# Moving six waits and taking the second block's norm squares to ScalarE in a two-block float32 kernel

## The reference

```
h = rms_norm(first_block(x));  h = layer_norm(h, ln_in)
for l in 0, 1:
    h = layer_norm(ALPHA * h + mixer(h), ln1[l])
    h = layer_norm(ALPHA * h + peer(h),  ln2[l])
layer_norm(x): mu = mean(x); var = mean((x - mu)^2); (x - mu) * rsqrt(var + 1e-5) * g + b
```

## Time and profile before

| | |
|---|---|
| median of 3 runs | 3114.88 us (3111.44 to 3116.8) |
| profiled execution | 3113.87 us |
| its span, first to last instruction | 3111.7 us |
| TensorE matmul busy | 3059.2 us, 98% |
| VectorE busy | 2120.8 us, 68% |
| ScalarE busy | 1488.1 us, 48% |
| GpSimd busy | 419.5 us, 13% |
| mean granted TensorE clock | 0.996 |
| DMA | 579.6 MB, mean 186 GB/s |

### The profile page before, as it was taken

The page is one execution under the profiler, slowest core; times in us unless marked ns, Lnnn a source line. Parts: engine busy times, 40 slices in busy tenths (PEclk is TensorE's granted clock), DMA queues, the critical chain, the costliest instruction groups (busy, mean ns, idle before and its releaser), DMA issues.

```text
span 3111.7 us, 59223 instructions
## 1 busy us (share of the span) xinstructions
PE 3059.2 (98%) x21073; PEld 2793.1 (90%) x21073; DVE 2120.8 (68%) x3732; ACT 1488.1 (48%) x2326; POOL 419.5 (13%) x246
## 2 busy tenths in 40 slices
PE   8999999999999999999999999999999999999998
PEld 8998899999888997899999978887899999988886
DVE  5567555555756557669788767776759977867776
ACT  4455444444644444444454445454434454545543
POOL 0001000000011002038700000001108810000000
PEclk9999999999999999999999999999999999999999
DMA  6543255455333553457765677774447765577775
GB/s 226 184 154 116 95 171 188 163 186 186 121 102 133 186 188 113 159 177 227 219 189 185 199 240 240 243 240 162 156 149 219 229 199 182 184 240 241 240 243 178
DMA packets 213024, 579.60 MB, mean 186 GB/s; under 512 B 23744, under 2 KB 88544, under 8 KB 212368
## 3 DMA queue, kind: packets, MB, share of 16 engines
q1 hardware_dynamic: 209504, 563.67, 54.8%
q0 software_dynamic: 3376, 13.94, 1.4%
HBM read 541.34 MB, written 36.18 MB: 186 GB/s over the span
## 4 chain that ended last, share of the span: by engine, by line
PE 87%; POOL 4%; DVE 4%; issue 3%; DMA 1%; ACT 1%; SPq 0%; POOLq 0%; ACTq 0%; DVEq 0%
PE work L667 40%; PE acc L690 33%; POOL wsp L640 3%; PE acc L752 3%; PE acc L1222 3%; PE acc L1089 2%; DVE wsp L417 1%; PE work L1123 1%; PE work L890 1%; PE work L904 1%; PE work L680 1%; DMA back<-acts_dram 0%; PE work L1010 0%; DVE st L2043 0%; PE work L816 0%
## 5 line engine op out<-in xcount | busy, mean ns | idle before, releaser
L667 PE MATMUL work<-xsp,wsp 128*128 128x256 f32 x12096 | 1502.5, 284 | 0.7 <-DVE wsp L417 0.7
L667 PEld LDWEIGHTS work<-xsp,wsp 128*128 128x128 f32 x12096 | 1472.2, 192 | 10.7 <-issue 3.0
L417 DVE TENSOR_TENSOR wsp<-ring,wsp 128x1024 fp32r<-128x1024 f32 x824 | 1011.8, 1229 | 569.1 <-ACT wsp L414 568.3
L414 ACT ACTIVATE wsp<-ring 128x1024 fp32r<-128x1024 f32 x944 | 994.3, 1054 | 648.1 <-PE work L667 352.3
L690 PE MATMUL acc<-wsp,hsp 128*128 128x512 f32 x4128 | 954.3, 390 | 4.6 <-DVE hsp L2312 4.4
L690 PEld LDWEIGHTS acc<-wsp,hsp 128*128 128x128 f32 x4128 | 770.3, 188 | 162.8 <-issue 6.2
L640 POOL TENSOR_TENSOR wsp<-ring,wsp 128x1024 fp32r<-128x1024 f32 x120 | 306.1, 2562 | 159.7 <-ACT wsp L414 159.5
L1611 ACT ACTIVATE hsp<-arena 128x256 fp32r (+1 forms) x256 | 107.1, 418 | 355.2 <-PE acc L690 337.1
L542 POOL TENSOR_TENSOR st<-st,mhalf 128x1 f32<-128x1 f32 x24 | 21.8, 908 | 1603.2 <-DVE st L1684 817.0
L2274 DVE TENSOR_TENSOR one_hots<-iota,selT 128x512 bf16<-128x512 bf16 x256 | 97.2, 422 | 81.8 <-PE acc L1222 81.7
L2312 DVE TENSOR_TENSOR hsp<-arena,hsp 128x256 fp32r<-128x256 f32 x256 | 108.9, 425 | 57.0 <-ACT hsp L1611 57.0
(11 more groups left out here) (322 smaller groups left out, 1938.2 us busy)
## 6 DMA issues: line engine op xcount, KB each, us to landing
ring<-in_stream SPq DMA_DIRECT2D x944, 512.0 KB, 3.4
back<-acts_dram SPq DMA_DIRECT2D x252, 128.0 KB, 3.1
acts_dram<-acts SPq DMA_DIRECT2D x128, 128.0 KB, 3.6
acts_dram<-arena SPq DMA_DIRECT2D x124, 128.0 KB, 4.1
rows_sb<-in_rows POOLq DMA_DIRECT2D x10, 512.0 KB, 6.3
h_saved_dram<-h POOLq DMA_DIRECT2D x2, 1024.0 KB, 5.0
h<-h_saved_dram POOLq DMA_DIRECT2D x2, 1024.0 KB, 6.0
scratch<-in_levels POOLq DMA_DIRECT2D x3, 448.0 KB, 4.4
```

What stands on the lines that cost most here:

```text
L414: self.eng.activation(dst[:, 0, :], src, ACT.Copy).then_inc(high_done, 1)
L417: self.eng.tensor_tensor(dst[:, 1, :], src, dst[:, 0, :].bitcast(F32), ALU.subtract)\
L667: mm = pe.matmul(out_, lhsT=w[:, a, 128 * c:128 * c + 128], rhs=xsp[:, b, c, :], start=(c == 0 and n == 0), stop=(c == DC - 1 and n == 2))
```

## The change

1. **peer, SP queue:** `act_back` 2 and 3 are issued before `load` of V.u + 4.
2. **mix1, ScalarE:** the eviction of `ttq1` 0 (with its split) goes ahead of the two exponentials of `dec`; `ttq1` 1 stays behind them.
3. **peer, TensorE:** instead of waiting for query tiles 12 to 15, heads 6 and 7 each wait for their own two.
4. **mix2, ScalarE and VectorE:** both split `tt.u + 4` before ScalarE's Exp and Ln and VectorE's scan.
5. **mix2, VectorE:** K.u + 16 is split, then `xsp_lows` of `yT0`, then K.u + 17.
6. **mix2, GpSimd queue:** `wa` is loaded first, on a semaphore of its own, for which alone ScalarE waits; TensorE waits for the rest ahead of the `wgu` matmuls.
7. **Norms of the second block:** the sum over columns comes from an accumulator output of the adding (or multiplying) VectorE instruction; the mean's negative is one small instruction; ScalarE squares (h - mean) with an accumulator output; the variance is one small instruction per block, the second of them between block 0's two long products. `bn_stats` and `bn_aggr` go. `busy` goes from 60, 40, 40, 40 to 51, 29, 29, 29.

```diff
@@ sync
-                load(U.u + ahead + SPILLED)
                 for s in range(4):
                     sp.wait_ge(acts_slot[s], 16 * (l + 1) * spills(s))
                 sp.wait_ge(unit_done, V.u)
                 act_back(l, 2)
                 act_back(l, 3)
+                load(U.u + ahead + SPILLED)
                 load(U.u + ahead + SPILLED + 1)
@@ gpsimd
                 pool.wait_ge(side_free, l + 1)
+                pool.dma_start(wa_sb, wa[l]).then_inc(ev("wa_in"), 16)
                 pool.dma_start(swt_sb, swt[l]).then_inc(side_in, 16)
                 pool.dma_start(masks, levels[0:LEVELS].rearrange("n p t -> p n t")).then_inc(side_in, 16)
-                pool.dma_start(wa_sb, wa[l]).then_inc(side_in, 16)
@@ tensor, mix2
-                X = make_xT(part, h, "xT", ("ln_ready", 2 * l + 1), busy=40 if l else 60)
+                X = make_xT(part, h, "xT", ("ln_ready", 2 * l + 1), busy=29 if l else 51)
-                pe.wait_ge(side_in, 16 + 64 * (l + 1))
                 pe.wait_ge(ev("wa_low"), l + 1)
...
                         G.claim(pe, 0)
+                        pe.wait_ge(side_in, 16 + 48 * (l + 1))
@@ tensor, peer
-                X = make_xT(part, h, "xT", ("ln_ready", 2 * l + 2), busy=40)
+                X = make_xT(part, h, "xT", ("ln_ready", 2 * l + 2), busy=29)
-                for q in range(12, 16):
-                    G.freed(pe, q)
+                queries = G
...
+                        if b == 0 and i >= 6:
+                            queries.freed(pe, 2 * i)
+                            queries.freed(pe, 2 * i + 1)
@@ scalar
+            def ln_squares():
+                for b in range(NB):
+                    act.wait_ge(ev("mean_ready"), NB * normed[0] + b + 1)
+                    act.activation(xs[:, b, :], h[:, b, :], ACT.Square, bias=moments[:, b, 0:1], accum_out=st[:, b:b + 1])\
+                       .then_inc(ev("sumsq"), 1)
+                normed[0] += 1
@@ scalar, mix1
+                channel("ttq1", 0, 2)
                 for q in range(2):
                     G.freed(act, q)
                     act.activation(dec[:, 2 * q:2 * q + 2], dec[:, 2 * q:2 * q + 2], ACT.Exp)\
                        .then_inc(ev("dec_exp"), 1)
-                for q in range(2):
-                    channel("ttq1", q, 2 + q)
+                channel("ttq1", 1, 3)
@@ scalar, mix2
-                act.wait_ge(side_in, 16 + 64 * (l + 1))
+                act.wait_ge(ev("wa_in"), 16 * (l + 1))
...
                     if q == 1:
+                        split.upto(G.u + 4)
                         act.wait_ge(ev("zabs_ready"), l + 1)
@@ vector, add_block
+                    if sums:
+                        ins = stt(hs, hs, scale_h, ACC[2 * b + n][:, :], ALU.mult, ALU.add,
+                                  accum_out=st[:, 4 + 2 * b + n:5 + 2 * b + n])
@@ vector, layer_norm
+                    if part is None:
+                        scaled()
+                        ins = stt(h[:, b, :], h[:, b, :], st[:, 2 + b:3 + b], final_row, ALU.mult, ALU.mult,
+                                  accum_out=st[:, 4 + 2 * b:5 + 2 * b])
+                        step(ins)
+                        ins = ts(moments[:, b, 0:1], st[:, 4 + 2 * b:5 + 2 * b], -1.0 / D, None, ALU.mult)
+                    else:
+                        add_block(b, last, 1.0, ALPHA, True)
...
-                    for m in range(2):
-                        ins = dve.bn_stats(st[:, 12 * b + 6 * m:12 * b + 6 * m + 6], h[:, b, 512 * m:512 * m + 512])
-                    step(ins)
-                    step(dve.bn_aggr(moments[:, b, :], st[:, 12 * b:12 * b + 12].rearrange("p (m s) -> p m s", m=2)))
-                    ts(moments[:, b, 1:2], moments[:, b, 1:2], EPS2, None, ALU.add).then_inc(ev("square_ready"), 1)
+                        ins = ts(moments[:, b, 0:1], st[:, 4 + 2 * b:5 + 2 * b], st[:, 5 + 2 * b:6 + 2 * b], -1.0 / D,
+                                 ALU.add, ALU.mult)
+                    ins.then_inc(ev("mean_ready"), 1)
+                def variance(b):
+                    norms[0] += 1
+                    dve.wait_ge(ev("sumsq"), norms[0])
+                    ts(moments[:, b, 1:2], st[:, b:b + 1], 1.0 / D, EPS2, ALU.mult, ALU.add)\
+                        .then_inc(ev("square_ready"), 1)
+                variance(0)
+                dve.wait_ge(ev("mean_ready"), NB * normed[0])
                 for b in range(NB):
                     hb = h[:, b, :]
-                    step(stt(hb, hb, moments[:, b, 0:1], rows[:, 0:1024], ALU.subtract, ALU.mult))
+                    step(stt(hb, hb, moments[:, b, 0:1], rows[:, 0:1024], ALU.add, ALU.mult))
+                    if b == 0:
+                        variance(1)
@@ vector, mix2
-                split.upto(A.u + 3)
+                split.upto(A.u + 4)
                 dve.wait_ge(ev("lg_ln"), l + 1)
...
+                split.upto(K.u + 16)
+                xsp_lows(part, "yT0", yg[:, l, :], 0, 4, ysp)
                 split.upto(K.u + 17)
-                xsp_lows(part, "yT0", yg[:, l, :], 0, 4, ysp)
```

More of the change, by code:

```diff
@@ L1287, in squares @@
                        .then_inc(ev("sumsq"), 1)
+            normed = [0]
+            def ln_squares():
[4 more added lines that the diff above has]
+                normed[0] += 1
             def ffn(part, l, gain, before):
@@ L1569, in mix2 @@
                 split.upto(Group(part, "wout").u + DC + 1)
+                ln_squares()
             def peer(part, l):
@@ L1708, in _, with add_block @@
             blocks = [0]
-            def add_block(b, last, scale_acc, scale_h):
+            def add_block(b, last, scale_acc, scale_h, sums=False):
                 G, i = last
@@ L1718, in add_block @@
                     hs = h[:, b, 512 * n:512 * n + 512]
-                    if scale_h == 1.0:
+                    if sums:
+                        ins = stt(hs, hs, scale_h, ACC[2 * b + n][:, :], ALU.mult, ALU.add,
+                                  accum_out=st[:, 4 + 2 * b + n:5 + 2 * b + n])
+                    else:
                         ins = stt(hs, ACC[2 * b + n][:, :], scale_acc, hs, ALU.mult, ALU.add)
-                    else:
-                        ins = stt(hs, hs, scale_h, ACC[2 * b + n][:, :], ALU.mult, ALU.add)
                 ins.then_inc(acc_free if b else ev("h_first"), 1)
@@ L2031, in mix1 @@
                 add_to_h(part, (Group(part, "wout1"), 3), 1.0, 1.0)
+            normed = [0]
             def layer_norm(n, part=None, last=None):
+                normed[0] += 1
                 for b in range(NB):
-                    if part is not None:
-                        add_block(b, last, 1.0, ALPHA)
+                    if part is None:
[4 more added lines that the diff above has]
+                        ins = ts(moments[:, b, 0:1], st[:, 4 + 2 * b:5 + 2 * b], -1.0 / D, None, ALU.mult)
+                    else:
+                        add_block(b, last, 1.0, ALPHA, True)
                         if b == 0:
@@ L2041, in layer_norm @@
                             h_added(dve, part)
-                    for m in range(2):
-                        ins = dve.bn_stats(st[:, 12 * b + 6 * m:12 * b + 6 * m + 6], h[:, b, 512 * m:512 * m + 512])
-                    step(ins)
-                    step(dve.bn_aggr(moments[:, b, :], st[:, 12 * b:12 * b + 12].rearrange("p (m s) -> p m s", m=2)))
-                    ts(moments[:, b, 1:2], moments[:, b, 1:2], EPS2, None, ALU.add).then_inc(ev("square_ready"), 1)
+                        ins = ts(moments[:, b, 0:1], st[:, 4 + 2 * b:5 + 2 * b], st[:, 5 + 2 * b:6 + 2 * b], -1.0 / D,
+                                 ALU.add, ALU.mult)
+                    ins.then_inc(ev("mean_ready"), 1)
+                if part is None:
+                    dve.memset(st[:, 31:32], 0.0).then_inc(side_free, 1)
+                def variance(b):
[5 more added lines that the diff above has]
+                dve.wait_ge(ev("mean_ready"), NB * normed[0])
                 dve.wait_ge(rows_in, 32 * (n + 1))
@@ L2163, in mix2 @@
                 dve.memset(st[:, 31:32], 0.0).then_inc(rows_free, 1)
-                dve.wait_ge(side_in, 16 + 64 * (l + 1))
+                dve.wait_ge(side_in, 16 + 48 * (l + 1))
                 dve.memset(swt_sb[64:128, :, 0:64], 0.0).then_inc(ev("sgv_ready"), 1)
+                split.upto(K.u + 16)
+                xsp_lows(part, "yT0", yg[:, l, :], 0, 4, ysp)
                 split.upto(K.u + 17)
-                xsp_lows(part, "yT0", yg[:, l, :], 0, 4, ysp)
                 G = Group(part, "sgu")
@@ L2348, in _ @@
             dve.wait_ge(side_in, 16)
-            for b in range(NB):
-                scaled()
-                ins = stt(h[:, b, :], h[:, b, :], st[:, 2 + b:3 + b], final_row, ALU.mult, ALU.mult)
-            step(ins)
-            dve.memset(st[:, 31:32], 0.0).then_inc(side_free, 1)
             layer_norm(0)
```

## The result

The changed kernel takes 3083.45 us (median of 4 runs, 3081.71 to 3084.42), the kernel before on the same chip 3115.18 us (4 runs, 3111.44 to 3116.8): a ratio of 0.9899, 95% interval 0.9882 to 0.9916. The profiled execution took 3081.71 us, its span is 3079.8 us, 31.9 us shorter than the span before. In the profile TensorE's matmuls are 3042.8 us, 99% of the span (98% before); VectorE is busy 2107.1 us, ScalarE 1500.8, GpSimd 417.6.

What follows compares the result with a forecast made beforehand. TensorE, its matmuls filling 98% of the span, was taken as the bound. Five waits 12.9, norms 11.3, edit 6 2.0 and clock 4.1 make 30.3 us off 3113.87: 3083.6, as median 3085, range 3079 to 3097.

Steps and rivals of the forecast that it cites:

- edit 1, with its clock: Between the tables, both layers: earlier `back` 2 and 3 remove TensorE's whole 4.4 us wait, plus 1.7 us of half clock.
- edit 2, with its clock: mix1, both layers: second `gkk` pair comes 1.5 us earlier, 3.0 in sum, plus 1.2 us of half clock each.
- edit 3: Peer: 12 matmuls of heads 0 to 5 cover the copying out of the last query tile, gaining 1.4 us.
- edits 4 and 5: mix2: earlier low part of the first `tok` unit gains 2.2 us; `sgu` bank free one split earlier gains 1.9.
- edit 6: mix2, split transposes: low parts start earlier with `wa` first, 2.0 us for both layers, between 1.4 and 2.6.
- norms: Second block's norms: 2.2 us gained four times and 2.5 in the first, 11.3 in all, an accumulator read taken as 0.10.
- 2.90 + 4c: Norm: us from first adding instruction to first long product, c being one accumulator read; 3.30 at c 0.10.
- the next wait takes over: Rival: waits 0.5 to 1 us behind each removed one, half-clock stretches stay or move; 3095 us, chance 0.20.
- Roots starve: Rival: GpSimd's root waits behind VectorE's products, five norms lose 0.4 us each, edit 6 gives nothing; 3089 us, chance 0.13.
- Half rate of the accumulating product: Rival: first norm's two products take 1.07 us more each, 2.1 off the gain; 3087 us, chance 0.07.
- No difference: Rival: reads and semaphore waits cost what `bn_stats` did, half the waits go; gain 6 or less, 3109 to 3115, chance 0.03.
- slower: Rival: SP's queue order makes the V loop wait once per unit; at 0.2 us each 3135 us, chance 0.03.

Runs made afterwards that it cites:

- runs 6 to 8: Changed kernel with parts undone: edit 1 (3087.07 us), edit 6 (3087.37 us), edits 4 and 5 (3088.31 us), in that order.
- run 5: The changed kernel again, unaltered, timed beside three versions with edits undone: 3086.76 us, ratio 0.9899 to the kernel before.
- waits alone: Kernel before with edits 1 to 6 only, its norms and unread matmuls as they were: 3094.62 us, ratio 0.9927.
- run 10: Changed kernel with the reload of `h` and rows later, and both first products of each norm ahead of both second ones: 3084.91 us, ratio 0.9898.
- Run 9: Changed kernel with GpSimd's reload of `h` and the norm rows issued only after the twelfth V unit: 3085.45 us, ratio 0.9901.
- first execution: Profiled execution of the changed kernel in its first measurement, nothing altered: 3081.71 us, span 3079.8 us.
- run 2: Kernel before with the new norms and fewer unread matmuls only, edits 1 to 6 undone: 3101.59 us, ratio 0.9946.
- run 7: Changed kernel with edit 6 undone (`wa` issued third, one semaphore for all four loads): 3087.37 us.

## Why the prediction was right, point by point

The predicted 3085 us is 1.6 above the median, and 30.3 us were forecast for the profiled execution against 31.9 of span. The terms, by the stages above and runs 6 to 8, were less even than the sum. Edits 2 and 3 were not undone by themselves; theirs are differences of stages.

| term | forecast us | shown us |
|---|---|---|
| edit 1, with its clock | 4.4 + 1.7 | 5.0 (none of layer 0's 4.0 in run 5) |
| edit 2, with its clock | 3.0 + 2.4 | 0.7 and 2.3 |
| edit 3 | 1.4 | 1.0 (both U stages, waits alone; within their spread) |
| edits 4 and 5 | 4.1 | 4.9 |
| edit 6 | 2.0 | 5.3, some 2.2 of it clock |
| norms | 11.3 | 12.6 |
| sum | 30.3 | 31.8 |

**Norms, right and mis-sized by 1.3.** The read of the accumulator was put at 0.10 us. The row says 0.08, but it starts before the product's row ends: by the prediction's own formula the first product starts 2.90 + 4c after the first add, and it starts 1289.95 - 1286.91 = 3.04 after it, so c is 0.035, an estimate as good as the 2.90. The last product then comes at 7.31 instead of 7.56. The prediction's 13.2 us for free reads is a slip: its formulas give 4 x 2.57 + 2.66 = 12.9, which moves no bound by more than 0.3 us. The root of block 0 is on the path, as predicted, and holds VectorE up for 0.25 us; run 10 takes it off and gets 0.33 and 0.37 us in the two mix2 stages. TensorE's wait for the norm grew to 1.0, not 1.3.

**Edit 1, the step that failed in part.** "They are there by 1789 even with a landing in 5 us" counts 5.4 us from the first unread matmul (1783.65). The issue came as forecast, 1769.86 - 1769.60 = 0.26 us behind it instead of 4.72 before. But the landing took 6.8 and 7.4 us, and tile 2 was used at 1776.65, 7.05 behind it and after 1.58 us of waiting for the DMA; TensorE still waits 0.77 us there and 0.6 and 0.4 in layer 1. The kernel before used its tile 2 at 1792.71, 9.06 behind, so of a head start of 4.5 us only 2.0 arrived. The prediction priced SP's order and took a landing time from issues that stood 7 us behind the reload of `h` (1781.19); edit 1 puts them 3 us behind it, into its transfer. The DMA share is 0.9 and more there. Run 9 shows that it is the reload, and also that moving it doesn't pay. One thing that the working rests on was told wrongly ahead of it: a V unit is 12 matmuls (6 for each block), not 24, as 4128 matmuls of L690 for 256 V units and 88 of the feed-forwards say. The prediction's 24 matmuls for two units are right.

**Edit 2.** The wait of 1.5 us at the first `gkk` pair is gone in both layers. The stage of mix1, from the unread matmuls ahead of it to the next, is 2.3 us shorter in layer 1 and 0.7 in layer 0. The half-clock stretch that stood at 252 to 260 is now, in the first execution, at 248, in front of the place where the wait had been: `ttq1`'s 48 matmuls take 7.50 us there and 6.01 in layer 1, and behind them L846 doesn't wait at all. That isn't edit 2's doing: run 2, which has not got it, shows the same `247.25 7.50` and a wait of 0.36 us at L846. In run 5 this stretch is absent and L846 and the matmuls behind it wait 0.54 and 0.52 us instead, and the whole stage is as long (191.9 against 192.0 us), so it costs nothing. Run 10 has such a stretch in layer 1, from 830, at the same price (190.8 against 190.7 us). But a second one, at 264 to 272, is in every trace that has edit 2 and in neither of the two that have not (before, run 2), with TensorE busy without a gap since 257 us; with it the stage of layer 0 is 1.2 us longer than layer 1's (192.0 against 190.7). This is the part of "the next wait takes over" that came true, though without a wait. Why this one comes in layer 0 and not in layer 1 stays open.

**Edit 6 and the stretches left standing.** The wait in the transposes fell from 2.0 to 0.83 us in layer 0. `wa` took 2.1 us to land where 3.7 was assumed, so it was there before the norm's end, and VectorE's low parts start 1183.02 - 1172.54 = 10.48 us after the first product. In layer 1, for which 11.1 was forecast, it is 2130.45 - 2120.47 = 9.98 from the norm's first instruction, and the wait there fell from 2.2 to 0.51 us. The clock's two stretches at the start of mix2, which the prediction left in place because 1.3 + 1.1 us of standing remain, are gone; their 1.4 each was priced, but for the range alone. The prediction puts half-clock stretches behind waits of 1.5 us and more and passes over the sixth of them, 2.05 us, which has none. So edits 4 to 6 gave 4.1 us more than forecast and the norms 1.3, and edits 1 to 3 gave 3.9 less. That the sum came within 1.6 us is in part luck: errors of 3.9 and 5.4 us went opposite ways, and executions of one kernel lie up to 4.6 us apart.

**The rivals.** *Roots starve*: no, the issue behind both roots goes out at 1177.94, before the third product starts. *The next wait takes over*: not for edits 3 to 6; for edit 1 in part, 1.7 of 4.4 us still being waited. *Half rate of the accumulating product*: 1.28 us with the accumulator and 1.28 without, so this pitfall of the Trainium skill (Vector Engine (DVE) Microarchitecture Reference, 7. Points that are easy to get wrong) isn't met by this form at float32. *No difference* and *slower*: the V loop runs 333 of 333 us busy at full clock.

## What to carry to other kernels

A wait in front of the bound engine costs its own length and puts its clock at risk: of the six waits of 1.5 us and more in the kernel before, five had a half-clock stretch behind them and one had not. Where the drop came back with one of them (layer 1 of run 7), the wait grew by 1.8 us and the stage by 3.9. When the cover of a stretch is filler work, cut the filler by as much as the stretch gets shorter, or the gain stays in the filler. And before a transfer is issued earlier, add up what all queues have in flight at that moment: here an issue 4.5 us earlier fell into another queue's 2 MB and brought the tile 2.0 us earlier. Last, read small edits stage by stage, and only in stages that repeat: two traces of one kernel differed by 4.8 us, nearly all of it in one stage.

## What the runs showed of the hardware that was not expected

A VectorE instruction's accumulator is read by an instruction of its own, 0.08 us long, which overlaps the end of the one that it reads: 0.035 us on the path, by the estimate above. Transfers of 128 KB on SyncE's queue landed in 6.1 to 8.0 us when issued 3 us behind 2 MB on GpSimd's queue, in 2.0 to 2.2 without those, and in 5.6 instead of 3.1 when issued 0.54 instead of 1.05 us ahead of them. The same kernel on the same chip has executions of 3082.62 and of 3087.19 us; the traced one of 3086.69 shows where 4.6 us can go: a tile that VectorE waited 7.36 us for instead of 4.31, and the half-clock stretch behind it. Nearly the same wait, 2.17 and 2.27 us, was followed by full clock in one layer and by half clock in the other, and the clock also fell with no wait before it.
